# Moving the buffers of a matmul-dense two-network kernel within 512 bytes of SBUF address

## What is computed

```
def swiglu(x, w_in, w_out):                      # 8 times in all
    a, b = jnp.split(x @ w_in, 2, axis=-1)       # w_in: 1024 x 5632
    return (jax.nn.silu(a) * b) @ w_out          # w_out: 2816 x 1024
...
x = x + 0.5 * swiglu(rmsnorm(x, ffn1_norm[l]), w_ffn1_in[l], w_ffn1_out[l])
u = rmsnorm(x, mix_norm[l])
c_q, c_kv, ... = split_sizes(u @ w_in[l], IN_SPLITS)
...
merged = gates[:, :, 0] * y_mla + gates[:, :, 1] * y_hg + gates[:, :, 2] * y_mem
x = x + merged @ w_out[l]
```

## The kernel before

| buffer | role in float32r matmuls | before | after |
|---|---|---|---|
| `UH` | moving | 416 | 448 |
| `UL` | moving | 0 | 448 |
| `HH`, `HL`, `MH`, `ML`, `OTH` | moving | 448 | 448 |
| `OTL`, `NAH`, `NAL` | moving | 128 | 448 |
| `MEMH`, `MEML` | moving | 128 | 128 |
| `WH`, `WL` of place 0 | weights | 0 | 0 |
| of place 1 | weights | 256 | 0 |
| of place 2 | weights | 320 | 0 |
| of places 3, 4, 5 | weights | 128 | 256 |
| of places 6, 7 | weights | 448 | 0 |
| `U` (plain float32) | moving | 416 | 416 |
| `V`, `RSTD`, `COS`, `SIN`, `SILU`, `TMP` | mostly none | 416 | 0 |
| `REGION`'s start | mixed | 448 | 448 |

## Time and profile before

### The profile page before, as it was taken

The page is one execution under the profiler, slowest core; times in us unless marked ns, Lnnn a source line. Parts: engine busy times, 40 slices in busy tenths (PEclk is TensorE's granted clock), DMA queues, the critical chain, the costliest instruction groups (busy, mean ns, idle before and its releaser), DMA issues.

```text
span 2843.6 us, 51128 instructions
## 1 busy us (share of the span) xinstructions
PE 2787.0 (98%) x21992; PEld 2650.6 (93%) x21992; DVE 1843.8 (65%) x3008; ACT 1298.9 (46%) x1860; POOL 70.7 (2%) x66
## 2 busy tenths in 40 slices
PE   8999999999999999999999999999999999999998
PEld 8999799999999879999999887899999998878998
DVE  5668576665666766766666557666666654766665
ACT  5445454444444545444444334444464433544443
POOL 0000000000000010000000001100000000110000
PEclk9999999999999999999999999999999999999999
DMA  7554356555555445555565653355555565435553
GB/s 257 177 173 130 111 173 202 181 179 192 185 175 166 117 148 178 174 182 182 193 204 166 189 145 116 93 182 188 183 174 183 173 195 140 134 90 167 180 187 109
DMA packets 481280, 474.50 MB, mean 167 GB/s; under 512 B 47104, under 2 KB 464416, under 8 KB 480928
## 3 DMA queue, kind: packets, MB, share of 16 engines
q1 hardware_dynamic: 477472, 460.75, 50.5%
q0 software_dynamic: 3584, 10.49, 1.4%
HBM read 464.91 MB, written 6.29 MB: 166 GB/s over the span
## 4 chain that ended last, share of the span: by engine, by line
PE 91%; DVE 5%; ACT 2%; DMA 1%; issue 1%; SPq 0%; DVEq 0%; ACTq 0%
PE ps L951 34%; PE ps L1050 33%; PE ps L1071 16%; PE ps L1188 2%; PE ps L1112 2%; PE ps L1157 1%; DVE WL L1881 1%; PE ps L998 1%; ACT WH L1502 1%; PE ps L1002 1%; PE ps L994 1%; DMA RAW<-in_w_in 0%; PE ps L982 0%; DMA RAW<-in_w_branch 0%; DVE REGION L2036 0%
## 5 line engine op out<-in xcount | busy, mean ns | idle before, releaser
L1881 DVE TENSOR_TENSOR WL<-RAW,WH 128x2048 fp32r<-128x2048 f32 (+2 forms) x390 | 871.4, 2240 | 409.3 <-ACT WH L1502 407.3
L1502 ACT ACTIVATE WH<-RAW 128x2048 fp32r<-128x2048 f32 (+2 forms) x398 | 736.8, 1865 | 153.4 <-DMA RAW<-in_w_in 81.7
L1071 PE MATMUL ps<-HH,WH 128*128 128x256 f32 x1408 | 391.5, 278 | 0.0
L1071 PE MATMUL ps<-HH,WL 128*128 128x256 f32 x1408 | 391.4, 278 | 0.0
L1071 PE MATMUL ps<-HL,WH 128*128 128x256 f32 x1408 | 391.3, 278 | 0.0
L951 PE MATMUL ps<-UH,WH 128*128 128x256 f32 x1328 | 381.5, 287 | 3.8 <-DVE WL L1881 3.8
L1050 PE MATMUL ps<-UH,WH 128*128 128x256 f32 x2688 | 373.5, 281 | 0.7 <-DVE WL L1881 0.7
L951 PE MATMUL ps<-UH,WL 128*128 128x256 f32 x1328 | 373.0, 281 | 0.0
L951 PE MATMUL ps<-UL,WH 128*128 128x256 f32 x1328 | 372.4, 280 | 0.0
L1050 PE MATMUL ps<-UL,WH 128*128 128x256 f32 x2688 | 372.2, 281 | 0.0
L1050 PE MATMUL ps<-UH,WL 128*128 128x256 f32 x2688 | 371.4, 280 | 0.0
(11 more groups left out here) (326 smaller groups left out, 3707.0 us busy)
## 6 DMA issues: line engine op xcount, KB each, us to landing
RAW<-in_w_ffn_in SPq DMA_DIRECT2D x88, 1024.0 KB, 5.1
RAW<-in_ffn_wi SPq DMA_DIRECT2D x88, 1024.0 KB, 5.0
RAW<-in_w_in SPq DMA_DIRECT2D x86, 1024.0 KB, 5.2
RAW<-in_w_ffn_out SPq DMA_DIRECT2D x32, 1024.0 KB, 4.8
RAW<-in_ffn_wo SPq DMA_DIRECT2D x32, 1024.0 KB, 4.8
RAW<-in_w_out SPq DMA_DIRECT2D x16, 1024.0 KB, 4.8
RAW<-in_w_ffn_out SPq DMA_DIRECT2D x16, 768.0 KB, 4.2
RAW<-in_ffn_wo SPq DMA_DIRECT2D x16, 768.0 KB, 4.1
```

The source lines that it names most:

```text
L1071: last = nc.tensor.matmul(bank(n + side, 0, T), a[:, k, side * P:(side + 1) * P], b[:, k0 + k, :], start=k0 + k == 0 and a is wh and b is ...
L1502: nc.scalar.activation(split_ap(s, part_high(s)), raw_ap(s), ACT.Copy).then_inc(weights_high, 1)
L1881: v_.tensor_tensor(split_ap(s, part_low(s)), raw_ap(s), split_ap(s, part_high(s)).bitcast(FP), ALU.subtract)\
```

## The change

Pads are computed instead of written out, so that `UH`, `UL` and `REGION` start at 448 modulo 512 and the weight buffers of places 0 to 2 at 0. The offsets of the overlays move by 32 words for places 3, 4 and 5, and by 16 words for places 6 and 7; those of `OTL`, `NAH` and `NAL` move too. 32 unused words stand between `BQ` and `CQ2`, because place 3 now ends 32 words later. The table above has the results: places 3 to 5 end up at 256, not 0, and `MEMH` and `MEML` stay at 128. On every engine the same instructions stand in the same order with the same waits.

```
-GAPS = (24, 64, 16, 24)
-OVERLAYS = {3: 11312, 4: 15408, 5: 19504, 6: 0, 7: 4096}
+OVERLAYS = {3: 11344, 4: 15440, 5: 19536, 6: 16, 7: 4112}
+ROUND, MOVING, STILL = 512, 448, 0
...
-        UH = sb("UH", [P, DK, T], FR)
-        sb("GAP_L", [P, GAPS[0]])
-        UL = sb("UL", [P, DK, T], FR)
+        def gap(name, place):
+            words = (place - (nc.sbuf_base + 31) // 32 * 32) % ROUND // 4
+            if words:
+                sb(name, [P, words])
+        gap("GAP_U", MOVING)
+        UH, UL = sb("UH", [P, DK, T], FR), sb("UL", [P, DK, T], FR)
+        gap("GAP_W", STILL)
         raw, low, high = [], [], []
         for i in BASE:
-            if i:
-                sb(f"GAP{i}", [P, GAPS[i]])
             at = (nc.sbuf_base + 31) // 32 * 32
...
-        sb("GAP_V", [P, GAPS[3]])
         V = sb("V", [P, T])
...
+        gap("GAP_R", MOVING)
         region_base = (nc.sbuf_base + 31) // 32 * 32
...
-        OTH, OTL = overlay("OTH", [P, 4, T], 2 * DK * T), overlay("OTL", [P, 4, T], TAIL)
+        OTH, OTL = overlay("OTH", [P, 4, T], 2 * DK * T), overlay("OTL", [P, 4, T], TAIL + 80)
-        NAH, NAL = overlay("NAH", [P, 4, T], 12336), overlay("NAL", [P, 4, T], 13360)
+        NAH, NAL = overlay("NAH", [P, 4, T], 12288), overlay("NAL", [P, 4, T], 13312)
...
-        BQ, CQ2 = region(4, T), region(4, T)
+        BQ = region(4, T)
+        region(32)
+        CQ2 = region(4, T)
```

## The result

The changed kernel has a median of 2804.79 us (2790.36 to 2812.12, 4 executions) against 2845.45 us (2844.68 to 2846.97, 4 executions) on the same chip: a ratio of 0.9849, interval 0.9824 to 0.9875. That is 40.7 us faster where 58.7 were forecast, inside the range and outside the forecast's own (2777 to 2803): it lies in the band that was left open for another rival, the order of products. What no part of the prediction speaks of is the scatter: 2 us before, 22 us after.

A forecast was written before the change was run, and what follows sets the result against it. PE, busy 98%, bounds the kernel by matmul count times pace. Terms of 66.3 us, less slabs staying slow (61.7) and 3 us taken back, gave 58.7: 2845.7 - 58.7 = 2787 us, range 2774 to 2819.

The forecast's parts named there:

- the forecast's own: Range for the case of a fast pace in all three matmul loops, 2777 to 2803 us, chance 0.72.
- the order of products: Rival: L1050's own walk through the weights keeps it at the slow 117.7 ns; about 2818 us, half way 2803; chance 0.18.
- The rule of the Trainium skill: Rule against the change: TensorE's independent read ports never wait, so buffer addresses cannot matter; worth 0 us, 2845.7.
- The 109.2 ns: The skill's issue gap for 256 columns, N/2.4 + 2.5 ns, taken to hold whatever the address.
- a slow pace that persists: Rival: with all starts alike nothing restores the fast pace; all float32r matmuls at 117.8 ns, 2853 us; chance 0.06.
- L1050: Term for the networks' first half: 8064 matmuls from 118.0 to 113.6 ns, gaining 35.5 us.
- L1071: Term for the networks' second half: 4224 matmuls at 115.3 ns on average, 1.7 ns less each, gaining 7.2 us.
- The deduction for slabs that stay slow: Across the float32r loops, 2/29 of matmuls keep the old pace, cutting the gain from 66.3 to 61.7 us.
- Between the networks: L951 products 18.7 us, OT, M and NA parts 3.4, opening slabs 1.5, less 3 taken back by other engines.
- Cover of DVE and ACT: In the networks, DVE's 28 us of cover in 85 hides slower starts, and supply keeps up, DVE rising from 67% to 69%.

The follow-up runs named there:

- the stream alone: A kernel with only float32r matmuls over pairs of starts, no other engine at work, against no kernel: most pairs 116.5 to 120.2 ns, others 113.3 to 113.5.
- the second stream: Float32r matmuls alone, behind waits, detours and alternations of starts, against no kernel: (448, 0) fast behind waits in 47 of 48 cases, slow after detours in 17 of 64.

## Why the prediction was right, and where its size was off

The sign and the cause held. The pace depends on the pair of starts, PE at 98% passes it on to the time, and L1050 took the fast pace at its new starts in its own order of products. The rule of the Trainium skill ("SBUF — State Buffer", "Who interferes with whom") by which the time would not move is not borne out: the ratio is below 1, and in the stream alone nothing but the starts differs between 113.3 and 118.5 ns. What fails is what the prediction drew from it, that the pace cannot depend on the address; on whether PE ever waits for another engine, which is the other half of it, the stream says nothing. The 109.2 ns that the prediction sets beside it are given there for a single matmul by itself, not for a stream with weight loads, for which no run here shows less than 113.3.

That the time is inside the range is in part luck. The forecast with its own range missed it by 2 us, and the room up to 2819 had been made for the case that L1050 keeps the slow pace by its order of products, which did not occur. Most of the 18 us that the forecast lacks come from a slow pace that persists, priced there as a case for all matmuls at once and put outside the range.

Term by term, in the profiled executions:

- L1050: forecast 35.5 us before the deduction, measured 23.7. The fast pace was sized right: 114.26 us for 1008 matmuls, forecast 114.5. Five networks gave 4.7 us each, the second and the sixth 0.2 each, and the fifth nothing.
- L1071: forecast 7.2, measured 2.3. (The stretches that the prediction adds up, 488.0 us for 4224 matmuls, give 115.5 ns and not 115.3; its term should have been about 1 us larger.) It went to 59.84 in five networks, forecast 60.0, and to 62.19 in three.
- The deduction for slabs that stay slow is the step that failed. I put "2/29 that stays slow", 4.6 us. It was three networks of eight in the first profile, five and four in the others, at 6.8 us each, or 2.3 for the fifth: 16 us in the first profile. I had counted slabs of before as if each drew for itself. In before the starts change every few slabs, and these changes bring the fast pace back; the change took them away. I wrote that down as a rival, "nothing may kick it any more", and gave it 0.06 as a case for all matmuls at once. It came true for part of the networks, in each execution others.
- Between the networks: forecast 18.7 + 3.4 + 1.5 - 3, measured 7.9. I had given its products the fast pace as a whole, but of the 3984 matmuls with `UH` and `UL` in L960 2496 ran fast, by the distance of their starts in the trace. Some 1.5 us went to the clock, which is 1.00 in the stretches that the prediction shows, but not throughout. Many of the products there are short, 24 matmuls, and stand between plain float32 ones. Behind such, a stream alone begins slow in 30 of 48 cases. That this is what holds L960 back is argued from that run; no version of the kernel tested it, and with one place at 128 these products are no faster (2256 of the 3984 in its first profile).
- Cover of DVE and ACT: right in seven networks, wrong in the fifth. Its first half is bound by the weights' coming, at 120.2 us before and after, so the 4.4 us that the prediction has for it were not to be had by addresses. That shows best with one place at 128, where nearly all other slabs of the networks are fast: the time is still 9 us above the forecast of 2787, and 5.4 of them are this stage (119.8 us against 114.4).

## What to carry to other kernels

When a kernel is bound by a stream of 256-column float32r matmuls with a weight load each, compare its pace slab by slab with the starts of its buffers modulo 256 bytes: 4% can hang on them, at no cost in instructions. Do not make all starts alike. Take a pair whose fast pace is stable, and let at least one weight buffer in the round have another such start (here 128 among 0, with the moving operand at 448), so that a stream that began slow is brought back within a few slabs. First look for stages that PE does not bound: a faster pace gives nothing there. If a change makes executions scatter where they did not, look for a state that is kept, and take more executions before a size is believed.

## What the runs showed of the hardware

- The pace of float32r matmuls of 128x256 with a load of 128 columns each is 113.3 ns at best, and 116.5 to 120.2 ns for most pairs of starts, with nothing else running, at a granted clock of 1.00.
- For some pairs, (448, 0) and (448, 128), 113.3 and 117.8 ns are both stable, over the 1536 matmuls of a network. Whether a stream at (448, 0) begins slow depends on what ran ahead of it: it does in 30 of 48 cases behind plain float32 matmuls, 1 of 48 behind a wait, 4 of 4 behind weights at 192, 17 of 64 behind a detour of 8 matmuls.
- A step of the weights' start from 128 to 0 modulo 256 brought a slow stream back to 113.3 ns in each of the six networks that began slow with one place at 128 (the fifth left aside). No stream of matmuls alone tested this step on a slow stream.
- The map of paces repeats modulo 256 bytes in both starts, but which of two stable paces is taken can differ between starts that are 256 apart: 117.9 against 113.3 ns at (448, 0) and (448, 256), behind 16 matmuls at (448, 320). As (448, 0) was fast behind the same 16 in 71 of 71 cases of the second stream, this is one more draw and no proof of a difference by 256 bytes.
- Why the pace depends on both starts, when each operand has a read port of its own by the Trainium skill ("SBUF — State Buffer", "Who interferes with whom"), stays open. No run here separates a conflict in the memory from one in PE's own front.
